# Attention in pairs of score tiles, probabilities divided in place and transposed, neighbourhood projections spread over one long attention

## The reference

```
# neighbourhood (nat), 16 heads of 64, 256 queries, 256 neighbourhood keys (masked) + 256 context keys
s_nb = q @ kw + bias ; s_cx = q @ kc
p = softmax(concat([s_nb, s_cx])) ; o = p_nb @ vw + p_cx @ vc
# differential (diff), 4 heads, causal, two score matrices of 64 each
w = softmax(q1 @ k1 * s + bias) - lam * softmax(q2 @ k2 * s + bias) ; o = w @ v
# block attention (moba), 4 heads of 128: with 256 tokens there is one block, so it is causal with bias
# latent attention (mla), 8 heads, q and k of 96, v of 64, causal
p = softmax(where(rel >= 0, q @ k * scale, -1e30)) ; o = p @ v
```

## Time and profile before

| | us |
|---|---|
| median of three runs | 3334.35 |
| the profiled execution | 3335.01 |
| its span | 3333.2 |
| PE busy in the span | 3189.2 |
| DVE busy | 1838.9 |
| ACT busy | 1167.0 |
| POOL busy | 62.3 |

### The profile page before, as it was taken

The page is one execution under the profiler, slowest core; times in us unless marked ns, Lnnn a source line. Parts: engine busy times, 40 slices in busy tenths (PEclk is TensorE's granted clock), DMA queues, the critical chain, the costliest instruction groups (busy, mean ns, idle before and its releaser), DMA issues. The chain is left out here.

```text
span 3333.2 us, 47025 instructions
## 1 busy us (share of the span) xinstructions
PE 3189.2 (96%) x19173; PEld 2758.7 (83%) x19173; DVE 1838.9 (55%) x3647; ACT 1167.0 (35%) x2007; POOL 62.3 (2%) x106
## 2 busy tenths in 40 slices
PE   7999999999989999999998999999989999999898
PEld 4788887888868888788887777999878999788898
DVE  1677654444458876533324434556556655655665
ACT  2322223233232222332223324444444444344443
POOL 1000000000000000000000000000001000001000
PEclk9999999999989999899998999999999999999999
DMA  8445542212226565433323222655225454324452
GB/s 263 114 137 170 150 161 64 66 61 83 70 64 180 191 191 176 133 90 106 94 82 94 63 63 69 195 168 187 77 89 177 152 183 133 114 89 140 139 189 90
DMA packets 501214, 421.36 MB, mean 126 GB/s; under 512 B 9946, under 2 KB 497674, under 8 KB 501000
## 3 DMA queue, kind: packets, MB, share of 16 engines
q1 hardware_dynamic: 497976, 412.33, 40.3%
q0 software_dynamic: 3024, 6.03, 0.7%
HBM read 417.20 MB, written 1.12 MB: 126 GB/s over the span
## 5 line engine op out<-in xcount | busy, mean ns | idle before, releaser
L1254 DVE TENSOR_TENSOR w_low<-raw,w_high 128x1024 fp32r<-128x1024 f32 (+2 forms) x720 | 761.9, 1100 | 358.5 <-ACT w_high L839 357.4
L839 ACT ACTIVATE w_high<-raw 128x1024 fp32r<-128x1024 f32 (+2 forms) x720 | 647.8, 948 | 689.3 <-PE gemm L1872 408.9
L1872 PE MATMUL gemm<-xh,w_high 128*128 128x512 f32 (+1 forms) x1792 | 675.9, 377 | 22.3 <-DVE xl L1290 22.3
L1872 PE MATMUL gemm<-xl,w_high 128*128 128x512 f32 (+1 forms) x1792 | 666.3, 372 | 0.0
L1872 PE MATMUL gemm<-xh,w_low 128*128 128x512 f32 (+1 forms) x1792 | 666.0, 372 | 0.0
L1872 PEld LDWEIGHTS gemm<-xh,w_high 128*128 128x128 f32 x1792 | 341.2, 190 | 94.2 <-issue 18.3
L1872 PEld LDWEIGHTS gemm<-xh,w_low 128*128 128x128 f32 x1792 | 341.3, 190 | 63.2
L1872 PEld LDWEIGHTS gemm<-xl,w_high 128*128 128x128 f32 x1792 | 341.9, 191 | 60.7 <-issue 0.7
L1872 PE MATMUL gemm<-yh,w_high 128*128 128x256 f32 x1216 | 353.6, 291 | 15.4 <-DVE yl L1315 7.1
L1872 PE MATMUL gemm<-yl,w_high 128*128 128x256 f32 x1216 | 348.1, 286 | 0.0
L1872 PE MATMUL gemm<-yh,w_low 128*128 128x256 f32 x1216 | 347.7, 286 | 0.0
(11 more groups left out here) (307 smaller groups left out, 4429.2 us busy)
## 6 DMA issues: line engine op xcount, KB each, us to landing
raw<-in_ffn_w_in SPq DMA_DIRECT2D x176, 512.0 KB, 5.2
raw<-in_w_mod SPq DMA_DIRECT2D x72, 1024.0 KB, 7.0
raw<-in_w_in SPq DMA_DIRECT2D x50, 1024.0 KB, 5.3
raw<-in_w_up SPq DMA_DIRECT2D x32, 1024.0 KB, 5.5
raw<-in_w_down SPq DMA_DIRECT2D x32, 1024.0 KB, 5.2
raw<-in_ffn_w_out SPq DMA_DIRECT2D x32, 768.0 KB, 4.5
raw<-in_ret_w_in SPq DMA_DIRECT2D x24, 1024.0 KB, 5.2
raw<-in_ffn_w_out SPq DMA_DIRECT2D x32, 640.0 KB, 4.1
```

The costliest lines, as they stand in the source:

```text
L839: act.activation(wh[i % SPL][:, a:b], raw[slot_of["w", i]][:, a:b], ACT.Copy).then_inc(w_high, 1)
L1254: dve.tensor_tensor(wl[slot][:, a:b], raw[slot][:, a:b], wh[i % SPL][:, a:b].bitcast(F32), ALU.subtract).then_inc(w_low, 1)
L1872: ins = pe.matmul(out, l_, r_, start=first and j == 0, stop=last and j == 2)
```

## The change

All attention now works on pairs: in neighbourhood and latent attention two heads, in block attention two heads, in differential attention the two score matrices of a head, each for 128 queries. There are 16 pairs in one neighbourhood attention (`nat`, no longer four), and per layer 8, 4 and 8 in the others. Each pair takes two steps.

- Scores: in neighbourhood and differential attention (`apart`) both products come first, then both biases, the two tiles in `aux[0]` and `aux[1]`, and the scores of the next pair wait for both exponentials. In the other two both tiles lie in one bank, and pairs alternate between two banks.
- The row maximum is negated by the reduction itself; with both tiles in one bank one reduction does both.
- DVE divides the exponentials in place (`divide`), in differential attention with the subtraction, so that one matrix is left. PE transposes them with the identity in transpose mode.
- The values of two heads that have 64 columns each are taken in turn, key tile by key tile; one copy and one subtraction per pair write the output.
- Neighbourhood masks are added by one instruction a head, into four buffers instead of two.
- The nine projection groups stand beside the one neighbourhood attention, one for every third half pair from the first on; the last seven half pairs have none. Scores and values of each four heads wait for the projections of these heads.

The diff, cut to its core:

```diff
+                upto = min(nb, (x + 2) // 3) if a.nat else 1 + x * (nb - 2) // na
...
     (ACT)
-                for j, (t, i) in enumerate(a.units):
-                    if j and a.units[j - 1][0] != t:
-                        turn_out(t - 1)
-                        if t >= 2:
-                            out_high(t - 2)
-                    if j + a.lead < n:
-                        exponentials(j + a.lead)
-                    yield 1
+                for p in range(n):
+                    if p + 1 < n:
+                        exponentials(p + 1, 0)
+                    if a.nat:
+                        if p:
+                            out_high(p - 1)
+                        turn_out(p, 0)
+                    if p + 1 < n:
+                        exponentials(p + 1, 1)
+                    if p and not a.nat:
+                        out_high(p - 1)
+                    yield 1
+                    turn_out(p, 1)
+                    yield 1
...
     (DVE)
-                    chain(dve.tensor_reduce(st_[:, 2, s8:s8 + 1], aux[u % 2][:, 0:k], AX.X, ALU.max))
-                    dve.tensor_scalar(st_[:, 0, s8:s8 + 1], st_[:, 2, s8:s8 + 1], -1.0, None, ALU.mult).then_inc(s_max, 1)
+                            dve.tensor_reduce(stat_of(a, p, 0, i), scores_of(a, p, i), AX.X, ALU.max,
+                                              negate=True).then_inc(s_max, 1)
...
+                    chain(dve.reciprocal(stat_of(a, p, 2), stat_of(a, p, 1)))
+                    if a.kind == "dif":
+                        chain(dve.tensor_scalar(second, second, stat_of(a, p, 2, 1), lamn[:, co:co + 1], ALU.mult, ALU.mult))
+                        dve.scalar_tensor_tensor(out=first_, in0=first_, scalar=stat_of(a, p, 2, 0), in1=second,
+                                                 op0=ALU.mult, op1=ALU.add).then_inc(p_scaled, 2)
+                    else:
+                        dve.tensor_scalar(first_, first_, stat_of(a, p, 2, 0), None, ALU.mult).then_inc(p_scaled, 1)
+                        dve.tensor_scalar(second, second, stat_of(a, p, 2, 1), None, ALU.mult).then_inc(p_scaled, 1)
...
+                for p in range(n):
+                    divide(p)
+                    if p + 1 < n:
+                        row_max(p + 1)
+                    if p:
+                        out_low(p - 1)
+                    yield 1
+                    if a.nat and p % 2 == 0 and 2 <= p < NH - 2:
+                        mask_bias(p + 2)
+                        mask_bias(p + 3)
+                    yield 1
...
     (PE)
+                    if a.apart:
+                        product(0)
+                        product(1)
+                        with_bias(0)
+                        with_bias(1)
...
-                                ins = pe.matmul(aux[2][:, P * kt:P * kt + P], pe_[:, uq % a.slots, P * kt:P * kt + P],
-                                                dg_[:, uq % a.slots, :], start=q == 0, stop=q == nu - 1)
+                            ins = pe.transpose(aux[2][:, P * kt:P * kt + P], probs_of(a, p, i)[:, P * kt:P * kt + P], ident)
...
+                    if a.kind in ("nat", "mla"):
+                        seq_ = [(i, kt) for kt in range(nkt) for i in range(2)]
...
+                for p in range(n):
+                    if p + 1 < n:
+                        scores(p + 1)
+                    if p:
+                        values(p - 1)
+                    turn(p, 0)
+                    yield 1
+                    turn(p, 1)
+                    yield 1
...
-            for g in range(4):
-                nxt = [f"nat_{k}{g + 1}" for k in "qkv"] if g < 3 else []
-                alongside(f"nat{g}", attention(f"nat{g}", f"nat_v{g}"), gemm, nxt)
+            alongside("nat", attention("nat"), both(*(gemm(f"nat_{k}{g}") for g in range(1, 4) for k in "qkv")))
```

More of the change, by code:

```diff
@@ L458, in program, with add_att @@
         atts = {}
-        unit_total = tile_total = 0
-        def add_att(name, tiles, bufs):
-            nonlocal unit_total, tile_total
+        pair_total = 0
+        def add_att(name, pairs):
+            nonlocal pair_total
             a = Att()
[L464 to L472, removed]
+            a.name, a.pairs, a.kind = name, pairs, name[:3]
+            a.p0 = pair_total
+            pair_total += len(pairs)
+            a.p1 = pair_total
+            a.nat = a.kind == "nat"
+            a.apart = a.kind in ("nat", "dif")
@@ L473, in add_att @@
             atts[name] = a
-        tiles = []
-        for hd in range(NH):
-            c, r = hd // 2, 64 * (hd % 2)
+        pairs = []
+        for c in range(NH // 2):
             for qt in range(2):
[L479 to L485, removed]
@@ L500, in program @@
-            add_att(f"diff{l}", tiles, B2)
-            tiles = []
-            for hd in range(DH):
+                    n, y0 = P * (qt + 1), P * (1 - qt)
+                    pairs.append(dict(
+                        units=[dict(qk=(q2[r:r + 64, hd, P * qt:P * qt + P], k2[r:r + 64, hd, 0:n]), rows=(0, P), col=0,
+                                    bias=(0, n, t5[:, hd, y0:y0 + n]), v=lambda k, hd=hd: v2[:, k, P * hd:P * hd + P])
+                               for r in (0, 64)],
+                        keys=n, layer=l, ov=aux[3][:, 0:P], out=oraw[:, hd, P * qt:P * qt + P]))
@@ L523, in program @@
-            add_att(f"mla{l}", tiles, B2)
+                    pairs.append(dict(
+                        units=[dict(qk=(mq[0:96, 2 * c + i, P * qt:P * qt + P], mk[0:96, 2 * c + i, 0:n]),
+                                    rows=(64 * i, 64 * i + 64), col=0,
+                                    bias=(P * qt, P * qt + P, cst[:, C_CAUSAL:C_CAUSAL + P]),
+                                    v=lambda k, c=c, i=i: mv[:, k, P * c + 64 * i:P * c + 64 * i + 64]) for i in range(2)],
+                        keys=n, ov=aux[3][:, 0:P],
+                        out=(ah[:, 8 + c, P * qt:P * qt + P], al[:, 8 + c, P * qt:P * qt + P])))
@@ L2218, in _ @@
                 pe.wait_ge(sub_t, DH * (l + 1))
-                for x in range(len(atts[f"moba{l}"].units)):
+                for x in range(2 * len(atts[f"moba{l}"].pairs)):
                     next(steps)
```

401 lines of the change are left out of this document (191 added, 210 removed).

## The result

The changed kernel takes 3237.6 us (median of 4 runs, 3237.1 to 3239.3) where the kernel before took 3335.0 beside it (3333.5 to 3337.5): a ratio of 0.9708, with a 95% interval of 0.9691 to 0.9725. That is 97.4 us saved, where 67 were forecast.

What follows compares the result with a forecast made beforehand. PE, busy 96% of the span, was taken as the bound; savings of 39 us in neighbourhood attention plus 2 x (2 + 2 + 10) in the layers made 67, so 3335 - 67 = 3268 us. Range 3240 to 3305, at 0.80.

Steps and rivals of the forecast that it cites:

- the whole overlap: Products and values on distinct row or column halves run wholly side by side: 48 us saved in neighbourhood attention, 3254 us.
- I take the middle: Neighbourhood pair's two products overlap partly: 1.5 us, between 1.05 side by side and 1.9 one after the other.
- The period of a pair: Neighbourhood pair with no projection near: 6.0 us for 8.1 before, 7.3 without overlap, 5.4 with whole overlap.
- Between projections: Neighbourhood time to the next projection: 6.2 us behind a first half, 10.1 behind a second, four of each, 65.2.
- Masks at nothing: Neighbourhood maskings sit two and a half pairs (15 us) behind their buffers' release, so they were costed at nothing.
- Transposes: Diagonal products in all attention become transposes: 248 products of 0.22 us become 224 transposes of 0.11.
- Differential heads: Differential attention: 6.1 us a head against 6.65, bound by the chain and not PE; 2 us a layer saved.
- Latent attention: Attention's own time falls from 31 to 21 us, as the low half is written earlier: 10 us a layer saved.
- (a): Rival: no overlap between row or column halves of PE; 39 us saved, 3296 us; chance 0.22.
- (b): Rival: each alternation of halves on PE costs 0.2 us; 3328 us; chance 0.06.
- (d): Rival: queue order binds more, ACT's copies hold PE in each pair, differential 1 us per head slower; 3311 us; chance 0.07.
- (c): Rival: PE's clock falls to 1.2 GHz in attention; 3343 us in neighbourhood alone, 3427 with other kinds; chance 0.05.

Runs made afterwards that it cites:

- run 11: Changed kernel with run 8's early masks, values between the two transpose groups, and ACT's copy of transposed probabilities ahead of both exponentials: 3231.10 us.
- run 8: Changed kernel with the neighbourhood masks of a later pair issued on DVE ahead of the odd half step's end, before a projection's evictions: 3236.95 us.
- run 3: Changed kernel with transposes made as plain float32 products with the identity, not in transpose mode: 3258.09 us.
- run 7: Changed kernel with, in differential heads alone, each bias straight behind its product and transposes as plain products: 3245.64 us.
- run 4: Kernel before the change, with DVE writing the low half ahead of the next tile's row maximum: 3315.87 us, ratio 0.994.
- run 1: Changed kernel with the values of a pair of heads taken head by head, not in turn: 3246.98 us.
- run 9: Changed kernel with run 8's early masks, values between the two transpose groups and the output copy last on ACT: 3230.46 us.
- run 10: Changed kernel with run 8's early masks, values between the two transpose groups, and the first head's transposed probabilities copied by DVE, not ACT: 3227.29 us.
- run 2: Changed kernel with each bias straight behind its product in neighbourhood and differential attention: 3282.57 us, ratio 0.9839.
- run 6: Changed kernel with each bias straight behind its product in the differential heads alone: 3252.42 us (runs from 3244.6 to 3259.9).
- run 12: Changed kernel with the neighbourhood projection groups spaced as before the change, three in eight half pairs from the third on: 3244.57 us.

## Why the prediction was off

The direction was right, and so were the mechanisms but for the differential heads; the sum was short by 30 us: neighbourhood 50.8 for 39, differential 5.5 and 7.2 for 2 and 2, latent 13.6 for 10 twice; block attention 2.4 and 1.2 for 2 and 2, and 3 us lie between and behind these stages. No single term carries it. By the prediction's own sum the whole overlap gives 3254, and 3237.6 is 16 us less, so three steps failed beside each other: the products at 1.5 us, the chain of copy and exponential in a pair, and the differential products at nothing.

- **The first step that failed: "I take the middle" (products of a pair 1.5 us).** The products of a pair on two row halves take 1.06 us, not 1.5, and all the values 1.03; one product took 1.05. The overlap is whole. The end "wholly side by side" stood in the text, and was not taken because no row showed it. The Trainium skill ("TensorE: Matmul & The Clock Gate", Part 3, packing small matmuls) says that matmuls on distinct row or column groups run side by side, and the trace agrees. 0.44 us in each of 16 pairs is 7 of the 11.8 us missed in the neighbourhood (an estimate that takes all of it to be on the path). That each product is two records in order was no evidence for half an overlap.
- **The period of a pair**: 6.0 forecast, 5.22 measured, the whole-overlap end being 5.4. The waited-for copy was named rightly (0.84 in eleven pairs). Of the 0.78 less, 0.4 is the scores. The rest is in the second step that failed, the chain behind them: first transposes to copy, copy to exponential and the exponential itself each took some 0.1 less than the 0.85, 0.59 and 0.88 of the sum, which added whole lengths where the rows overlap (0.76, 0.49 and 0.77 start to start).
- **Between projections**: 6.2 forecast, 5.5 measured for three of the four (6.99 for the one with the mask wait of 1.37), and 10.1 forecast, 8.78 measured, four times. The head took 6.4 for 8.5, the tail 18.6 for 19.3 with a mask wait of 1.11 in it. The 1.7 us put down for the half clock at the start did not come; that is partly luck, since the same stage had a mean clock of 0.62 over 4.5 us in run 11.
- **Masks at nothing**: wrong in two places, 2.5 us, because they stand behind a projection's evictions on DVE, not because a landing came late. Run 8 takes them away, and its total shows nothing of it.
- **Transposes** at 0.11 each against 0.22: right. Start to start they are what the earlier trace rows said, and run 3 prices them at 20.5 us for the whole change. The Trainium skill ("TensorE: Matmul & The Clock Gate", Terms) states four times for FP32; the trace shows twice, and the measurement decides.
- **Differential heads, the third step that failed**: 6.1 us forecast, 5.19 measured. The estimates of 3.5 and 2.6 for the two lengths of key were each 0.3 to 0.6 too long. The text said that PE "is not late there any more", so that the doubled products saved nothing. But the scores are the first link of the chain, behind the exponentials of the pair before. Runs 3 and 7 show it, both with plain transposes and at a clock of 1.00 in both layers: 39.25 and 39.07 us with the products first, 43.55 and 43.39 in order. The pairing of products carries 4.3 us a layer, and the rest of the change some 2.
- **Latent attention**: 16 us of PE were forecast and 59.34 - 45.47 = 13.9 measured, and waits of 3.4 for 4 to 5. The start was misread too: the text has 21 of PE and 10 of waits before, where the earlier trace rows give 23.0 and 7.9. The low half written earlier is worth 5.1 us in the old kernel (run 4), the transposes 2.2 in the new (run 3). If the two add, 6.3 of the 13.6 are left, and they are not split further; taking the values in turn has no part in them (run 1).
- **Rivals.** (a) and (b), no overlap or dear alternation, are refuted by the rows above. (d) is refuted for the differential heads, which got faster; ACT's copies do hold PE in each pair (0.84), and runs 9 and 10 show what that costs, 7 to 10 us. (c) did not happen in the changed kernel beyond a few us (1.00 in the neighbourhood, 0.96 in one differential stage, 0.94 in one of block attention), but runs 2, 6 and 12 show that it was near: one change of order brings the clock down to half for a part of a stage, and in run 6 the layer where it fell took 7.0 us longer than the other.

## What to carry to other kernels

Where the operands of two products sit on distinct row or column halves of PE, put the products next to each other and count one, not one and a half. Look behind each wait for what stands ahead in the releaser's queue before redesigning anything: one moved statement had 20 us in the old kernel, where the whole change has 97, and moving the values between two dependent groups of transposes had some 6 or 7 in the new. Price a step at both clock levels when PE's own work gets thinner: run 2 lost 24.8 us in the differential stages, where the same order costs 4.3 a layer at full clock (runs 3 and 7). And before a gain of 1 to 3 us is read off one profiled execution, compare the clock in the stages that nobody changed.

## What the runs showed of the hardware

- Two float32 products on row halves of PE: 1.06 us for both, 1.05 for one of 512 columns. On column halves sixteen records take 1.03 to the next instruction in turn; head by head that group is 0.49 longer, where wholly in line would be some 0.9, and in latent attention a group of eight records is no longer than in turn (0.66).
- The differential stage with its biases in order was at 0.77 in three of four profiled layers with transposes in transpose mode (0.96 in the fourth), and at 1.00 in four of four with plain products, which take twice the time and leave the stage faster.
- Executions of kernels that are the same up to the neighbourhood stage reached it at 1814.92 and 1819.62 us, at clocks of 0.98 and 0.97.
- Attention without projections kept the full clock over 18.7 us at the end of the neighbourhood stretch in the changed kernel, lost it in the last 2 us in run 8, and was at half in the last 8 of 24.7 in run 12.
- A copy of 512 columns out of PSUM: 0.68 us on DVE, 0.60 on ACT.
